# Seven products for the experts' gate projections: the sums moved among VectorE's work, the banks' roles changing by expert

## The reference, cut to what matters

```
for e in range(8):
    y = (silu(h @ w_gate[e]) * (h @ w_up[e])) @ w_down[e]     # 1024 -> 3584 -> 1024
    out = out + combine[..., e:e+1] * y
```

## Time and profile before

| | us |
|---|---|
| median of 3 runs (lowest, highest) | 1529.13 (1528.9, 1529.92) |
| the profiled execution's own time | 1528.53 |
| its span, first to last instruction | 1526.7 |
| TensorE busy in the span | 1508.6 |
| VectorE busy in the span | 921.5 |
| one expert of the middle, on TensorE | 106.33 |
| of that, in parts and down parts | 72.16 and 34.17 |

### The profile page before, as it was taken

One profiled execution on the slowest core, in us unless ns is written; L12 is line 12 of the kernel. 1 busy time (PEld: TensorE's weight loads), 2 busy tenths in 40 slices (PEclk: granted clock), 3 DMA queues, 4 the chain that ended last, 5 costly groups with the idle time before them and its releaser, 6 DMA issues.

```text
span 1526.7 us, 27999 instructions
## 1 busy us (share of the span) xinstructions
PE 1508.6 (99%) x11888; PEld 1033.6 (68%) x11888; DVE 921.5 (60%) x1533; ACT 497.4 (33%) x741; POOL 25.3 (2%) x39
## 2 busy tenths in 40 slices
PE   9999999999999999999999999999999999999997
PEld 7887788888888878843466566565565665664664
DVE  7778776888787776643824835726528339248211
ACT  5698745444457987420020110100100100201001
POOL 0000000000000000010000000000000000000100
PEclk9999999999999999999999999999999999999999
DMA  9544376555554444499999999999999999999994
GB/s 385 177 162 164 116 248 207 186 184 182 194 179 149 155 166 146 141 364 425 425 410 425 425 417 425 418 416 425 418 420 426 413 425 424 412 425 416 422 425 183
DMA packets 72673, 478.10 MB, mean 313 GB/s; under 512 B 8097, under 2 KB 8353, under 8 KB 45154
## 3 DMA queue, kind: packets, MB, share of 16 engines
q1 hardware_dynamic: 68656, 460.09, 75.8%
q0 software_dynamic: 3456, 15.72, 2.7%
q10 hardware_dynamic: 434, 0.45, 0.1%
HBM read 471.38 MB, written 4.85 MB: 312 GB/s over the span
## 4 chain that ended last, share of the span: by engine, by line
PE 85%; ACT 6%; DVE 5%; DMA 2%; issue 1%; SPq 0%; ACTq 0%; DVEq 0%
PE bank L1508 24%; PE mid L1508 12%; PE turn L1536 11%; PE bank L1233 7%; PE bank L1239 7%; PE bank L1242 7%; PE mid L1536 4%; PE mid L1233 2%; PE mid L1239 2%; PE mid L1242 2%; PE turn L1570 2%; ACT w_hi L586 1%; DVE w_lo L593 1%; DMA wide<-in_e_down 1%; PE mid L1345 1%
## 5 line engine op out<-in xcount | busy, mean ns | idle before, releaser
L1508 PE MATMUL bank<-wide,gT 128*32 128x448 f32 x3624 | 438.5, 539 | 0.0
L1508 PEld LDWEIGHTS bank<-wide,gT 128*32 128x32 f32 x3624 | 221.4, 110 | 131.6 <-issue 22.6
L593 DVE TENSOR_TENSOR w_lo<-raw,w_hi 128x1024 fp32r<-128x1024 f32 x202 | 244.4, 1223 | 93.0 <-ACT w_hi L586 90.6
L1508 PE MATMUL mid<-wide,gT 128*32 128x448 f32 x1824 | 254.2, 539 | 0.0
L586 ACT ACTIVATE w_hi<-raw 128x1024 fp32r<-128x1024 f32 (+1 forms) x202 | 210.2, 1053 | 101.1 <-PE bank L1242 65.5
L1145 ACT ACTIVATE eh<-bank 128x448 f32<-128x448 f32 x48 | 22.6, 544 | 478.3 <-PE bank L1508 478.3
L1536 PE MATMUL turn<-wide,hT 128*32 128x512 f32 x534 | 176.8, 592 | 1.4 <-DVE sums_w L2140 1.4
L1233 PE MATMUL bank<-w_hi,a_hi 128*128 128x512 f32 (+1 forms) x608 | 164.6, 394 | 0.8 <-ACT a_hi L869 0.8
L2219 DVE TENSOR_TENSOR eh<-mid,eh 128x448 f32<-128x448 f32 x32 | 19.8, 620 | 241.2 <-PE mid L1508 241.2
L1508 PEld LDWEIGHTS mid<-wide,gT 128*32 128x32 f32 x1824 | 115.5, 110 | 66.4 <-issue 12.8
L1242 PE MATMUL bank<-w_lo,a_hi 128*128 128x512 f32 (+1 forms) x608 | 157.1, 381 | 2.1 <-DVE w_lo L593 2.1
(11 more groups left out here) (313 smaller groups left out, 1985.0 us busy)
## 6 DMA issues: line engine op xcount, KB each, us to landing
wide<-in_e_in SPq DMA_DIRECT2D x227, 896.0 KB, 12.4
wide<-in_e_down SPq DMA_DIRECT2D x102, 1024.0 KB, 13.6
raw<-in_stream SPq DMA_DIRECT2D x100, 1024.0 KB, 4.8
extra<-in_e_in SPq DMA_DIRECT2D x23, 896.0 KB
extra<-in_e_down SPq DMA_DIRECT2D x10, 1024.0 KB
raw<-in_e_in SPq DMA_DIRECT2D x6, 896.0 KB, 4.5
wg<-in_gates POOLq DMA_DIRECT2D x2, 2048.0 KB, 10.5
table<-y_rows POOLq DMA_DIRECT2D x7, 384.0 KB
```

The costliest lines, as they stand in the source:

```text
L593: nc.vector.tensor_tensor(w_lo[:, h % H, :], raw[:, part % R, lo:lo + HALF], w_hi[:, h % H, :].bitcast(F32), ALU.subtract).then_inc(lo_rea ...
L1508: ins = nc.tensor.matmul((early, late)[m][t_][strip(r), 0:LANE_W], gT[:, kt, strip(t_)], w_[:, r * LANE_W:(r + 1) * LANE_W], start=kt == 0 ...
```

## The change

- Gate parts of experts 0 to 6 are taken in pairs (kt even and odd). Token groups 1 and 2 go through the same seven-product form: the 448 columns of a strip are cut into two sides of 224, and seven groups of four matmuls of 224 columns take the place of eight. Group 3 keeps its full 448 columns.
- VectorE makes T1, T3, T2 and T4 of each gate pair, as four instructions of 896 columns, in two of the four buffers. There are eight gate pairs for each expert. It makes four sums of the gathered tokens for each expert (`gathered_sums`).
- The seven products stand in five banks and are put together for each unit: ScalarE copies two half banks, and VectorE does five additions (`combine_gate`), after which silu reads group 1 and 2 from SBUF.
- As the gate now needs five banks, gate, up and down change banks between even and odd experts.
- The order of the in parts in a unit is now gate, gate, up, gate, up, gate, up, up (each a pair of parts), and the data in memory is laid out in that order. A gate pair counts its first part as used only after its product with T2.
- VectorE's order is rewritten: sums of a gate pair or a few pairs stand between all its other pieces, four down parts (two and two) are summed ahead of the second unit's products, and the sums of down parts 4 to 13 and of the next expert's first pair end the expert.

```diff
 
+IN_ORDER = ((0, 0), (0, 1), (1, 0), (0, 2), (1, 1), (0, 3), (1, 2), (1, 3))
+GATE_PARTS = 2 * (IN_ORDER.index((0, KT // 2 - 1)) + 1)
+SIDE = LANE_W // 2
+PAIRS_E = UNITS_E * KT // 2
+
+
 def expert_order():
 
-    out = [("in", u, kt + k, m) for u in range(UNITS_E) for kt in range(0, KT, 2) for m in range(2) for k in range(2)]
+    out = [("in", u, 2 * p + k, m) for u in range(UNITS_E) for m, p in IN_ORDER for k in range(2)]
     return out + [("down", d) for d in range(UNITS_E * UNIT_TILES // 2)]
...
-AHEAD = 3
+AHEAD = 4
+SLOTS_E = 2 * PAIRS_E + N_DOWN
+PAIR_AT = [E_ORDER.index(("in", u, kt, 0)) for u in range(UNITS_E) for kt in range(0, KT, 2)]
...
+        def gate_sets(n):
+
+            return [set_of(m)[:, j:j + 2, :].rearrange("p j f -> p (j f)")[:, 0:LANES * SIDE].rearrange(
+                "p (r f) -> p r f", r=LANES) for m in (n, n + 1) for j in (0, 2)]
+
...
+        def gate_banks(pas, e):
+            if not seven(pas, e):
+                return late if is_last(pas, e) else early
+            return (late[0], late[1], early[0], early[1], late[2]) if e % 2 else (turn[0], turn[1], *early)
+        def up_banks(pas, e):
+            if not seven(pas, e):
+                return early if is_last(pas, e) else late
+            return (turn[0], turn[1], early[2]) if e % 2 else late
+        def down_banks(e):
+            return late if e % 2 else (turn[0], turn[1], early[2])
...
-                        act.wait_ge(used, u0 + (u + 1) * UNIT_PARTS - 2 + e * E_PARTS)
+                        gates = gate_banks(pas, e)
+                        act.wait_ge(used, u0 + u * UNIT_PARTS + GATE_PARTS + e * E_PARTS)
+                        if seven(pas, e):
+                            k = e * UNITS_E + u
+                            if k:
+                                act.wait_ge(gate_sums, 5 * k)
+                            nc.scalar.activation(part_sum[:, 0, :], gates[2][:, 0:SIDE], ACT.Copy).then_inc(gate_copied, 1)
+                            nc.scalar.activation(part_sum[:, 1, :], gates[1][:, SIDE:LANE_W],
+                                                 ACT.Copy).then_inc(gate_copied, 1)
                         for n_, t_ in enumerate(BY_GROUP):
                             if not is_first(pas, e) or u:
                                 act.wait_ge(hT_turned, GROUPS_E * (q0 + u - 1) + n_ + 1 + e * (GROUPS_E * UNITS_E))
-                            nc.scalar.activation(eh[t_][:, :], early[t_][:, 0:LANE_W],
-                                                 ACT.Silu).then_inc(e_silu, 1)
+                            gate = gates[t_][:, 0:LANE_W]
+                            if seven(pas, e):
+                                if t_ < 2:
+                                    act.wait_ge(gate_sums, 5 * k + 4 + t_)
+                                gate = gates[4][:, 0:LANE_W] if t_ == 2 else eh[t_][:, :]
+                            nc.scalar.activation(eh[t_][:, :], gate, ACT.Silu).then_inc(e_silu, 1)
...
+                            if m == 0 and seven(pas, e):
+                                if kt == 0 and u:
+                                    pe.wait_ge(gate_sums, 5 * (e * UNITS_E + u))
+                                    pe.wait_ge(e_silu, GROUPS_E * (e * UNITS_E + u - 1) + 1)
+                                elif kt == 0 and e:
+                                    pe.wait_ge(e_hid, GROUPS_E * e * UNITS_E)
+                                g0, g1, g2, g3, g4 = gate_banks(pas, e)
+
+                                def four(place, h_, moving, opens=True, closes=True):
+                                    for r in range(LANES):
+                                        ins = nc.tensor.matmul(place[strip(r), :], h_, moving[:, r, :],
+                                                               start=opens and kt < 2, stop=closes and kt >= KT - 2)
+                                    return ins
+
+                                own_ = w_[:, 0:UNIT_W].rearrange("p (r f) -> p r f", r=LANES)
+                                first_side, second_side = own_[:, :, 0:SIDE], own_[:, :, SIDE:LANE_W]
+                                at0, at1 = slice(0, SIDE), slice(SIDE, LANE_W)
+                                a1, a2, a3 = (gT[:, kt, strip(t_)] for t_ in range(GROUPS_E))
+                                if kt % 2 == 0:
+                                    four(g2[:, at0], a1, first_side, closes=False)
+                                    four(g4[:, 0:LANE_W], a3, own_, closes=False)
+                                    continue
+                                n = slot_of(e, i - 1)
+                                t1, t3, t2, t4 = gate_sets(n)
+                                s1, s2, s3, s4 = (gS[:, j, kt // 2, :] for j in range(4))
+                                four(g0[:, at0], a1, first_side, closes=False)
+                                if kt == 1:
+                                    pe.wait_ge(x_sums, 4 * (e + 1))
+                                four(g2[:, at1], s4, second_side, opens=False)
+                                pe.wait_ge(w_second, n + 2)
+                                four(g3[:, at0], s3, t3)
+                                four(g1[:, at1], s1, t1, closes=False)
+                                four(g0[:, at1], s2, t2, opens=False).then_inc(used, 1)
+                                pe.wait_ge(w_sums, n + 2)
+                                four(g1[:, at0], a2, t4, opens=False).then_inc(w_sums_used, 2)
+                                four(g4[:, 0:LANE_W], a3, own_, opens=False).then_inc(used, 1)
+                                continue
                             if kt == 0 and not (is_first(pas, e) and u == 0):
                                 pe.wait_ge((e_silu, e_hid)[m], GROUPS_E * (q0 + u) + e * (GROUPS_E * UNITS_E))
+                            if kt == 0 and u == 0 and m == 0 and is_last(pas, e):
+                                pe.wait_ge(e_hid, GROUPS_E * e * UNITS_E)
                             if kt == 0 and u == 0 and m == 1 and pas == 0 and e:
-                                pe.wait_ge(row_act, ROW_ACT * (e - 1) + 3)
-                                pe.wait_ge(row_dve, ROW_DVE * (e - 1) + 1)
+                                pe.wait_ge(row_act, ROW_ACT * (e - 1) + (10 if seven(pas, e) else 3))
+                                pe.wait_ge(row_dve, ROW_DVE * (e - 1) + (3 if seven(pas, e) else 1))
+                            place = (gate_banks(pas, e), up_banks(pas, e))[m]
...
+                                if d == 0:
+                                    pe.wait_ge(gate_sums, 5 * (e + 1) * UNITS_E)
+                                    pe.wait_ge(e_silu, GROUPS_E * ((e + 1) * UNITS_E - 1) + 1)
+                                b0, b1, b2 = down_banks(e)
+                                n = slot_of(e, i)
+                                pe.wait_ge(w_second, n + 1)
+                                t1, t3, t2, t4 = (set_of(n)[:, j, :] for j in range(4))
...
+                def strip_sums(own_, place, ready, n):
...
+                def gathered_sums(e):
+
+                    if e == 0:
+                        dve.wait_ge(g_ready, 2)
+                    else:
+                        dve.wait_ge(g_turned, TURNED_G * e)
+                        dve.wait_ge(w_sums_used, (e - 1) * SLOTS_E + 2 * PAIRS_E)
+                    strip_sums(gT_of(pas, e)[:, :, :].rearrange("p (d c) t -> p d c t", c=2),
+                               [gS[:, j, :, :] for j in range(4)], x_sums, 4 * e)
+
...
+                def combine_gate(e, u):
...
+                    dve.wait_ge(gate_copied, 2 * (k + 1))
+                    if k:
+                        dve.wait_ge(hT_turned, GROUPS_E * k)
+                    nc.vector.tensor_tensor(pair(low[:, :]), pair(g0[:, 0:LANE_W]), twice(p1), ALU.add).then_inc(gate_sums, 1)
+                    nc.vector.tensor_tensor(c_, g2[:, SIDE:LANE_W], p5, ALU.add).then_inc(gate_sums, 1)
+                    dve.wait_ge(gate_sums, 5 * k + 1)
+                    nc.vector.tensor_tensor(b_, g3[:, 0:SIDE], low[:, SIDE:LANE_W], ALU.add).then_inc(gate_sums, 1)
+                    dve.wait_ge(gate_sums, 5 * k + 2)
+                    nc.vector.tensor_tensor(low[:, SIDE:LANE_W], low[:, SIDE:LANE_W], c_, ALU.add).then_inc(gate_sums, 1)
+                    dve.wait_ge(gate_sums, 5 * k + 3)
+                    nc.vector.tensor_tensor(pair(high[:, :]), pair(g1[:, 0:LANE_W]), twice(b_), ALU.add).then_inc(gate_sums, 1)
...
+                    def first_sums(i):
+
+                        n = slot_of(e, i)
+                        if E_ORDER[i][0] == "in":
+                            t1, t3, _, _ = gate_sets(n)
+                            if n >= SETS:
+                                dve.wait_ge(w_sums_used, n - SETS + 2)
+                            upper, lower_ = (weights_of(pas, i + j, e)[:, 0:UNIT_W].rearrange("p (r f) -> p r f", r=LANES)
+                                             for j in range(2))
+                            part_landed(dve, pas, i, e)
```

(54 more changed lines are left out.)

198 lines of the change are left out of this document (107 added, 91 removed).

## The result

The changed kernel takes 1535.48 us in the median of 6 runs (1534.41 to 1538.48) against 1529.03 before: a ratio of 1.0044, 95% interval 1.0031 to 1.0057. It is slower by some 6.5 us, 0.4%. I had said 1532.0 in a range of 1525.5 to 1546, and slower with a chance of 0.50 (the same 0.39).

A forecast was written before the change was run, and what follows sets the result against it. The weight stream was taken to bound the expert stage. Span 1526.7 + 1.4 + 0.5 + 1.1 = 1529.7; 1.8 above the span gives 1531.5, and 0.6 to the median 1532.1, stated as 1532.0 us, range 1525.5 to 1546.

The forecast's parts named there:

- The bound and TensorE's saving: Experts 0 to 6: the weight stream needs 107.36 us an expert, so TensorE's 21 us saved turn into idle time.
- Prices: Gate pairs: 0.376 us a group of four 224-column matmuls, 4.26 a lone pair's sums; VectorE busy 96 to 98 an expert.
- Rivals A and B: A: short matmul groups are slow, 1576 us, chance 0.08. B: VectorE's list bounds, 1550, 0.14 with longer chains like it.
- Rival C: The landed reserve is used and expert 7 starts up to 6.7 us earlier: 1522.5 us, half of it 1525 to 1526; chance 0.10.
- Term 3: Expert 6, landing of down part 0 to TensorE entering expert 7: 44.5 us instead of 43.4, +1.1, bounds -3.7 and +4.
- the cover of 2 us: Expert 6: TensorE could start down part 4 at 17.2 us after the landing, before VectorE's 19.2.
- Term 2: Gate pairs' extra instructions, 2688 plus some 400, mean 0.2 MB more instruction traffic: +0.5 us, bounds 0 and 1.
- Term 1: Expert 0's start: TensorE frees part 2 late, so the stream loses +1.4 us, kept to the end; upper bound 3.7.
- load 13: Weight load in expert 0 waiting for part 2: issued at 671.6, landing at 676.1 instead of 674.8, a loss of 1.3 us.
- touches: Small further stream losses at loads 17 and 21 in expert 0, taking 1.3 us to +1.4.
- five loads under way: Ring of weight buffers: TensorE's lag of five or six places leaves five loads, above the two needed, so the stream stays full.

The follow-up runs named there:

- filled wait: Changed kernel with seven unread 512-column matmuls, all in one strip, before TensorE's wait at down part 4 in experts 0 to 6: 1548.39 us.
- filled strips: Changed kernel with eight unread 512-column matmuls, two in each strip, before TensorE's wait at down part 4: 1536.4 us, ratio 1.0051.
- eighth back: Changed kernel with one of the seven products of every gate pair done twice, 21 us more TensorE work: 1537.36 us, ratio 1.0052.
- pair 1 first: Changed kernel with VectorE making gate pair 1's sums before turning the selection in expert 0: 1534.22 us, ratio 1.0033.
- all orders: Changed kernel with pair 1 first, unit 1's gate combined before the first down sums, gathered sums last, pair sums not interlaced: 1534.43 us.
- the saving alone: Kernel before with a quarter of group 2's gate product left out in experts 0 to 6, no VectorE sums added: 1528.1 us, ratio 0.9994.

## Why the prediction was right, and where it was off

**The bound and TensorE's saving: right.** The stream bounds the expert stage, and the 21 us are worth nothing that the runs can tell. Two experiments show it from both sides (0.9 us for taking them off alone, 1.9 for putting them back).

**Prices: right.** Groups of 224 columns at 0.38, a pair's sums and what is lost between them at 4.4 (4.26 said), VectorE busy 94.2 us an expert (96 to 98 said, so 2 less). Rivals A and B would have needed other rows. Rival C is refuted: nothing came earlier.

The Trainium skill (TensorE: Matmul & The Clock Gate, Part 1) has about 62 ns for each MATMUL where hardware decode is off. The trace of after doesn't show that bound: eight records of 224 columns in 0.38 us are 47 ns each.

**Term 3, the chain at expert 6: right.** 44.2 us against 44.5, and by the path that was said: TensorE starts down part 4 at 19.14 us after the landing (19.2 said), when VectorE's sum for it is there. The wait of 2.06 us at down part 0 and the lowered clock behind it were not in it: the first four parts took 11.2 us, where the stretch's mean in the earlier trace rows gives 9.8. They used up the cover of 2 us that I had given TensorE.

**Term 2, instruction traffic:** 0.18 + 0.04 MB more on two queues, as said; its price (+0.5) was not measured by itself.

**Term 1, the first expert: mis-sized.** It said +1.4 and counted load 13, with "touches" for the rest. Counted from the start of the gather, down part 0 lands 2.6 to 4.0 us later than before in four traces with this order (filled wait, filled strips, after, eighth back), and 1.6 to 2.0 us later in three with pair 1 first. So the term is about 3.3, inside the bound of 3.7 that it was given. The step that failed is the single load: after 667.81 no load goes out until 672.70 (671.6 said), and from there the stream runs on two or three loads fewer, at 310 GB/s instead of before's 389 for 10 us.

**What had no term: the stream in experts 1 to 6.** I said 107.3 to 107.4 us between landings throughout, gave a period off 107.4 as a sign of being wrong, and wrote that five loads under way keep the stream full. The six steps took 3.5 us more, two of them 109 us each. The mean lag was fine; what I didn't look at was the time without a release, up to 8.6 us instead of 4.5. By the rates, the two dips behind such gaps account for some 2.1 of the 3.5 us, and the rest lies mostly at the fetches of rows, where after dips lower than before (292 GB/s against 322 in the last).

Four things stay open here. Other gaps as long have no dip behind them. The two long steps end at 940.06 and 1371.48, while the dips come at 970 and 1185, so the dips don't explain which steps are long. No timed run shows what the dips are worth. And no run takes VectorE's sums off experts 1 to 6 with the rest left as it is, so why the fetches cost more isn't known.

The median's 6.5 us are then: some 3.3 in expert 0 (1.3 of which one reordered call gives back, with intervals that overlap), 0.8 in the chain, and some 2.4 for thinner loads and traffic, which is what is left and not measured. The forecast had 2.9 of the 6.5, from the right bound; that 1535.5 still lies inside the range is owed to a range made wide for the rivals, not to terms for these losses.

## What to carry to other kernels

Where TensorE and the stream are within a few per cent of each other, find the leader by who waits for landings, not by who is busiest, and price a change by what it does to the stream's releases. Here the mean lag hid that the stream would dip at all, and the longest gap between two releases didn't tell where (one of 8.3 us passed without a dip). An in-order engine that interlaces the next tile's first step with this tile's last one makes the last one wait for a landing; write it so only where the landing is sure to be early. Idle time of an engine that outruns the bound was moved by reordering here, not removed: three attempts gained nothing over the one reordering at the start.

## What was not expected of the hardware

- The granted clock fell to 0.57 of 2.4 GHz in the slice behind a wait of 2.45 us (852.5 to 855), so mostly to the lower level of 1.2, and stayed at 1.00 behind before's wait of 1.36 and behind waits of 0.71. The length of the wait alone doesn't decide it: the clock also stayed at 1.00 behind waits of 2.42 and 2.31 (eighth back, to 960.21 and 1284.05) and of 3.00 (all orders, to 955.42).
- Matmuls of 512 columns that follow each other in one strip of 32 columns go at 0.43 us a record; spread over four strips the kernel's own go at a quarter of that (a group of four, eight records, at 448 columns in 0.75 us). By the Trainium skill (TensorE: Matmul & The Clock Gate, Part 3) matmuls on different tiles of the array run at the same time; the filled strips agree: their 16 records took 1.93 us, the 14 in one strip 6.0.
- At an unchanged rate, the time from issue to landing tells how many loads are under way, and that is where a faster TensorE's time goes. Medians in us at the end of the row, in part loads and down part loads, of the kernel with the saving alone and of after (12.4 and 13.6 in the kernel before):

```profile
wide<-in_e_in SPq DMA_DIRECT2D x227, 896.0 KB, 16.1
wide<-in_e_down SPq DMA_DIRECT2D x102, 1024.0 KB, 18.9
```

```profile
wide<-in_e_in SPq DMA_DIRECT2D x227, 896.0 KB, 12.4
wide<-in_e_down SPq DMA_DIRECT2D x102, 1024.0 KB, 15.9
```

The same saving deepens the queue by 3.7 and 5.3 us when it comes free, and by 0 and 2.3 when each part must wait for VectorE's sums as well. No busy share shows this difference.
